# Two mixers' latent section merged into their input projection, with the results taken out of PSUM by ScalarE

## The reference, cut to what matters

```python
proj = h @ w_in                      # 1024 -> c_q 256, c_kv 128, k_r 32, f_q, f_k, f_v 512 each, f_logit 8
q  = (rms_norm(c_q, q_norm_g) @ w_uq).reshape(B, S, 8, 64 + 32)
kv = (rms_norm(c_kv, kv_norm_g) @ w_ukv).reshape(B, S, 8, 64 + 64)
q_rope = rope(q[..., 64:], positions);  k_rope = rope(k_r, positions)
log_f = log_sigmoid(f_logit + fox_forget_b);  F = cumsum(log_f, axis=1)
# then two causal attentions: MLA on q, kv, k_rope; FOX on f_q, f_k, f_v with F[q] - F[k] added
```

## Time and profile before

| | |
|---|---|
| median of 3 runs | 2799.9 us |
| the profiled execution: its own time, and its span | 2798.05 us, 2796.3 us |
| mean granted TensorE clock | 0.943 of full |
| busy: PE, DVE, ACT, POOL | 2484.0, 823.6, 288.8, 15.0 us |
| moved by DMA | 720.37 MB, mean 258 GB/s |

### The profile page before, as it was taken

One profiled execution on the slowest core, in us unless ns is written; L12 is line 12 of the kernel. 1 busy time (PEld: TensorE's weight loads), 2 busy tenths in 40 slices (PEclk: granted clock), 3 DMA queues, 4 the chain that ended last, 5 costly groups with the idle time before them and its releaser, 6 DMA issues. The chain is left out here.

```text
span 2796.3 us, 49835 instructions
## 1 busy us (share of the span) xinstructions
PE 2484.0 (89%) x22580; PEld 1559.8 (56%) x22580; DVE 823.6 (29%) x1418; ACT 288.8 (10%) x588; POOL 15.0 (1%) x12
## 2 busy tenths in 40 slices
PE   4679999977799999999999997799589729999996
PEld 3558888765534445354453534688489524444443
DVE  5672232346301110111011101355363342222222
ACT  1131000103100000000000001331121000000000
POOL 0100000010000000000000000000000000000000
PEclk8889999988799999999999998999699859999998
DMA  8527555503399999999999993333000048999995
GB/s 343 209 118 281 211 218 218 227 1 131 118 381 357 368 369 367 361 380 361 356 370 361 376 359 126 122 137 140 0 19 4 24 173 371 422 422 422 422 422 236
DMA packets 104664, 720.37 MB, mean 258 GB/s; under 512 B 11888, under 2 KB 12560, under 8 KB 29712
## 3 DMA queue, kind: packets, MB, share of 16 engines
q1 hardware_dynamic: 104464, 717.34, 64.8%
HBM read 716.21 MB, written 1.05 MB: 257 GB/s over the span
## 5 line engine op out<-in xcount | busy, mean ns | idle before, releaser
L1316 PE MATMUL bank<-ring,moe_xg 128*32 128x512 f32 (+1 forms) x6144 | 581.9, 539 | 6.1 <-DVE moe_acc L1427 5.5
L1316 PEld LDWEIGHTS bank<-ring,moe_xg 128*32 128x32 f32 x6144 | 198.0, 110 | 378.9 <-issue 368.6
L1340 PE MATMUL bank<-ring,moe_turned 128*32 128x256 f32 x5376 | 296.1, 379 | 0.0
L1340 PEld LDWEIGHTS bank<-ring,moe_turned 128*32 128x32 f32 x5376 | 172.5, 110 | 115.9 <-issue 4.4
L1545 PE MATMUL bank<-ring,moe_shared 128*64 128x512 f32 x1024 | 223.3, 594 | 0.9 <-DVE moe_shared L1599 0.9
L1000 PE MATMUL bank<-h_chan,ring 128*128 128x256 f32 x896 | 197.9, 382 | 3.8 <-ACT h_chan L444 3.8
L1000 PEld LDWEIGHTS bank<-h_chan,ring 128*128 128x128 f32 x896 | 171.8, 192 | 27.9 <-issue 4.1
L1907 PE MATMUL bank<-h_chan,ring 128*128 128x256 f32 x672 | 150.2, 384 | 4.5 <-DVE h_chan L2015 4.5
L1545 PEld LDWEIGHTS bank<-ring,moe_shared 128*64 128x64 f32 x1024 | 72.3, 137 | 142.9 <-issue 142.9
L1439 DVE TENSOR_TENSOR moe_hidden<-moe_silu,bank 128x512 f32<-128x512 f32 (+1 forms) x48 | 26.9, 616 | 400.6 <-PE bank L1316 400.6
L1907 PEld LDWEIGHTS bank<-h_chan,ring 128*128 128x128 f32 x672 | 128.7, 192 | 26.5 <-issue 9.1
(11 more groups left out here) (379 smaller groups left out, 2421.6 us busy)
## 6 DMA issues: line engine op xcount, KB each, us to landing
ring<-stream SPq DMA_DIRECT2D x313, 1024.0 KB, 12.4
ring<-wide SPq DMA_DIRECT2D x240, 1024.0 KB, 7.2
ring<-wide SPq DMA_DIRECT2D x128, 768.0 KB, 6.1
ada_slots<-stream SPq DMA_DIRECT2D x28, 1024.0 KB, 6.9
x_chan<-xT SPq DMA_DIRECT2D x1, 1024.0 KB, 14.7
ring<-lora SPq DMA_DIRECT2D x1, 1024.0 KB, 6.5
out<-x_chan SPq DMA_DIRECT2D x1, 1024.0 KB, 3.9
hyb_work<-dilated SPq DMA_DIRECT2D x1, 768.0 KB, 8.9
```

The costliest lines, as they stand in the source:

```text
L1316: mm = nc.tensor.matmul(banks[r][i * TILE:(i + 1) * TILE, 0:width], xg[:, t, r * TILE:(r + 1) * TILE], w[:, i, :], start=(t == 0), stop=(t ...
L1340: mm = nc.tensor.matmul(sum_bank[r][q * TILE:(q + 1) * TILE, :], turned[:, r, 4 * c + f, i * TILE:(i + 1) * TILE], w[:, f2, q * T:(q + 1) ...
```

## The change

Blocks 1 and 2 become one block. What moves:

- The slots UQ and UKV (query and key/value up-projections) take places 4 and 5 of the stage's stream; the projection's last four slots follow as 6 to 9.
- PE's order is a list of 34 items: 8 projection tiles, 8 query heads, 8 key heads, 2 value tiles, 8 projection tiles, rotating through 5 banks. The sums of squares follow item 4; a rotation product follows each of items 27 to 31, in 2 banks of its own.
- ACT empties all of these banks, and squares the latents straight from PSUM. In its fixed order it takes sine and cosine after item 1, the root after item 5, the forget gate's exponential and logarithm after item 7.
- DVE keeps the norm, the angles, the gate, the variances, the rotation and the modulation. Its modulation slots stand in groups: 0 and 1 behind the angles, 2 and 3 behind the latents' scaling, 4 to 7 behind the gate, 8 to 11 behind the rotation. The two reciprocals become one over 512 elements.
- SP issues positions first, then `c_row`, all mixer slots 2 to 9, modulation slots 4 to 7, the forget sums, modulation slots 8 to 11, and slots 10 to 13.
- POOL's four memsets stand at the start of the merged block.

The diff, cut:

```diff
-        banks = k.bank[1:7]
+        banks, rot_banks, lat_sums = k.bank[1:6], k.bank[6:8], k.bank[0]
+        items = [("tile", j, m) for j in range(4) for m in range(2)]
+        items += [("query", UQ, h) for h in range(HEADS)] + [("key", UKV, h) for h in range(HEADS)]
+        items += [("value", UKV, t) for t in range(TT)] + [("tile", j, m) for j in range(6, 10) for m in range(2)]
...
@@ SP
+                    for j in range(2, 10):
+                        loads.load(sp, j)
+                    for j in range(side.slots, 2 * side.slots):
+                        side.load(sp, j)
                 sp.wait_ge(*S("pool_step").at(2))
                 sp.wait_ge(*forget_step.at(4))
...
+                    for j in range(2 * side.slots, side.n):
+                        side.load(sp, j)
+                    for j in range(10, loads.n):
+                        sp.wait_ge(*side.done(side.n - side.slots + j - 10))
+                        loads.load(sp, j)
@@ PE
+                def turn(i):
+                    pe.wait_ge(*tile_out.at(10 + 2 * i if i < 4 else 4))
+                    if i >= 2:
+                        pe.wait_ge(*rope_ready.at(i - 1))
...
+                for n in range(len(items)):
+                    if n == 8:
+                        pe.wait_ge(*lat_ready.at(2))
+                    if n == 16:
+                        pe.wait_ge(*lat_ready.at(3))
+                    product(n)
+                    if n == 4:
+                        latent_sums()
+                    if 27 <= n < 32:
+                        turn(n - 27)
@@ ACT
+                for n, (kind, j, i) in enumerate(items):
+                    act.wait_ge(*item_done(n))
+                    b = banks[n % NB]
+                    if kind == "query":
+                        a(qm[0:96, i, :], b[0:96, 0:T], ACT.Copy, scale=96 ** -0.5).then_inc(*tile_out.up())
...
+                    elif j < 2:
+                        if n < 3:
+                            a(sq[:, n, :], b[:, 0:T], ACT.Square).then_inc(*lat_squares.up())
...
+                    if n == 1:
+                        act.wait_ge(*S("angle_ready").at(1))
+                        a(sin[:, :], sin[:, :], ACT.Sin)
+                        a(cos[:, :], cos[:, :], ACT.Sin).then_inc(*S("trig_ready").up())
+                    if n == 5:
+                        act.wait_ge(*lat_var.at(1))
+                        a(k.rstd[:, 0:2, :], k.rstd[:, 0:2, :], ACT.Sqrt).then_inc(*lat_root.up())
+                    if n == 7:
+                        act.wait_ge(*forget_step.at(1))
+                        a(e, e, ACT.Exp, scale=-1.0).then_inc(*act_step.up())
...
@@ DVE
+                dve.wait_ge(*S("small_arrived").at(16))
                 dve_angles(k, link, cos, sin, scratch[:, 0, :], scratch[:, 1, :], k.t("freq1"))
+                modulation(0, 1)
+                dve.wait_ge(*tile_out.at(4))
...
+                modulation(2, 3)
...
+                modulation(4, 5)
+                modulation(6, 7)
...
+                modulation(8, 9, 10, 11)
@@ the stream in HBM
+        head = slots_of(np.concatenate([cq, ckv, misc, fq, fk, fv], axis=1))
+        add(head[0:4])
...
+        add(head[4:8])
```

More of the change, by code:

```diff
@@ L564, in stage_mixer, with item_done @@
+        ends = [n + 1 == len(items) or items[n + 1][1] != items[n][1] for n in range(len(items))]
+        def item_done(n):
+            return loads.done(items[n][1]) if ends[n] else tile_done.at(n + 1 - sum(ends[:n]))
+        lat_squares, lat_sum, lat_var = S("squares_ready"), S("sums_ready"), S("var_ready")
+        lat_root, lat_ready = S("lat_root"), S("lat_ready")
+        rot_done, rope_ready = S("rot_done"), S("rope_ready")
         forget_step, forget_moved = S("forget_step"), S("forget_moved")
@@ L632, in _ @@
+                if side is not None:
+                    for j in range(2 * side.slots, side.n):
[3 more added lines that the diff above has]
+                        loads.load(sp, j)
+                loads.rest(sp)
+                sp.wait_ge(*forget_moved.at(32))
             @block.gpsimd
@@ new lines, in _ @@
+                v.scalar_tensor_tensor(e, z, 0.0, lo, ALU.max, ALU.subtract).then_inc(*forget_step.up())
+                dve.wait_ge(*lat_sum.at(1))
+                for g, width in enumerate((256, 128)):
+                    link(v.tensor_scalar(k.rstd[:, g, :], lat_sums[:, g * T:(g + 1) * T], 1.0 / width, EPS, ALU.mult,
+                                         ALU.add))
+                v.reciprocal(k.rstd[:, 0:2, :], k.rstd[:, 0:2, :]).then_inc(*lat_var.up())
+                dve.wait_ge(*lat_root.at(1))
@@ L666, in _ @@
-                n = 0
-                for h in range(HEADS):
-                    dve.wait_ge(*(head_done.at(h + 1) if h < HEADS - 1 else loads.done(8)))
-                    nc.vector.tensor_scalar(qm[0:96, h, :], k.bank[1 + n % 4][0:96, 0:T], 96 ** -0.5, None,
-                                            ALU.mult).then_inc(*head_out.up())
-                    n += 1
-                for h in range(HEADS):
-                    dve.wait_ge(*head_done.at(n))
-                    nc.vector.tensor_copy(km[0:64, h, :], k.bank[1 + n % 4][0:64, 0:T]).then_inc(*head_out.up())
-                    n += 1
@@ L676, in _ @@
-                for t in range(TT):
-                    dve.wait_ge(*(head_done.at(n) if t == 0 else loads.done(9)))
-                    nc.vector.tensor_copy(vm[:, t, :], k.bank[1 + n % 4][:, :]).then_inc(*head_out.up())
-                    n += 1
+                v.tensor_scalar(negF, F, -1.0, None, ALU.mult).then_inc(*forget_step.up())
+                modulation(4, 5)
+                modulation(6, 7)
                 dve.wait_ge(*S("trig_ready").at(1))
-                dve.wait_ge(*head_out.at(8))
```

260 lines of the change are left out of this document (104 added, 156 removed).

## The result

The changed kernel took 2734.53 us (median of 4 runs, 2730.73 to 2735.97) against 2800.97 for the kernel before on the same chip: a ratio of 0.9764, 95% interval 0.9747 to 0.9781. Run again later, 5 times, it took 2734.32, ratio 0.9765 (0.9752 to 0.9778). Forecast were 2730 and a range of 2720 to 2750. The profiled execution took 2735.66 us, its span is 2733.9 (62.4 us shorter), and the mean granted clock went from 0.943 to 0.953. By the medians the gain is 66.4 us: the profiled execution is one of the slower of the four.

What follows compares the result with a forecast made beforehand. Layer 1 was taken as bound by PE, then DVE's chain; layer 0 by SP's order, then the same chain. Gains of 28.4 + 2.4 + 38.7 = 69.5 us off 2798.05 gave 2728.6, as median 2730; range 2720 to 2750.

Steps and rivals of the forecast that it cites:

- PE is the bound of layer 1's merged block: Layer 1's merged block: PE's passes set its length, attention starts at 615.1 instead of 643.47, 28.4 us gained.
- The latents are ready in time: Before item 8 in both mixers: scaled latents ready ahead of PE, with 2.8 us to spare in layer 0, 3.1 in layer 1.
- The short prices of DVE's operations: DVE in the merged block: operations take short times, not 1.9 us beside a memset; otherwise layer 0 loses 1.2 us.
- Item 13 waits 0.6 us: Merged block: PE waits about 0.6 us for item 13's bank while ACT does exponential and logarithm with two table loads.
- The 11.9 us for slots go: Layer 0's projection: PE meets each weight slot as landed, so its 11.9 us of slot waits disappear.
- The rival in which positions and `c_row` wait for eight slots: Layer 0's transfers: both land with the eight slots, 21 us later, latents ready at 85, total 2748; chance 0.07.
- DVE's tail ends layer 0's block, 7 us late: End of layer 0's block: DVE's last four modulation slots end at 117.7, PE at 110.8; attention starts at 118.0.
- Attention of layer 1 gains 2.4 us from its clock: Layer 1's attention: PE arrives at full clock, first 16 passes take 3.5 us instead of 6.93; gain 2.4, bounds 0 and 3.5.
- The size of PE's path: Layer 1's merged block: projection tiles of 3.45 us each plus 17.3 us of passes pushed in between.
- Layer 0: Layer 0's merged block: attention starts at 118.0 instead of 156.77, 38.7 us gained.
- Later stages move as a whole: Dense and mixture stages: they start their loads in block 4, which moves as a whole; rival of no change, 2800, chance 0.02.
- ACT's reads free DVE of 15 us or more in each mixer, which the sums above already use: Both mixers: ACT's new PSUM reads take 15 us or more off DVE, already counted in the block estimates.

Runs made afterwards that it cites:

- the experiment with the spread tail: Changed kernel with layer 0's modulation slot 8 moved before the first rotation step and 9 to 11 between its steps: 2724.72 us, ratio 0.9728.
- the experiment with paired turns: Changed kernel with rotation products two after item 28, two after item 30, one after item 31, instead of one after each of items 27 to 31: 2735.76 us.
- ACT reads twice: Changed kernel with 30 additional reads of PSUM by ACT in each mixer: 2735.60 us, ratio 0.9772.

## Why the prediction was right, and where it was 7 us short

Forecast were 69.5 us off the profiled execution's time; measured were 62.4 (66.4 by the medians, so part of the 7 us is what runs of one kernel differ by). Point by point:

- *PE is the bound of layer 1's merged block.* Right. Item 8 began 535.15 - 503.25 = 31.90 us after PE's start, for which I had 570.1 - 538.2 = 31.9. The block saved 26.3 us instead of 28.4.
- *The latents are ready in time.* Right in both layers: the query latents were scaled at 64.9 in layer 0 and 532.1 in layer 1, 3.1 us before PE's first query head in either (forecast 2.8 and 3.1). The short prices of DVE's operations held.
- *Item 13 waits 0.6 us.* Right, 0.49 in both. By ACT's rows a table load of 1.28 us is followed by its operation after 0.01 (68.98, 70.27). The 5.6 us for table changes in the forecast's range are a term that no run shows; in its place the runs showed this 0.01 us and the wait of 0.49:

```profile
68.98 1.28 ACT L627 ACT_TABLE_LOAD   x1
70.27 0.42 ACT L627 ACTIVATE score<-score 8x256 f32<-8x256 f32 x1
```

- *The 11.9 us for slots go.* Right, and the order of SP is what removes them. The rival in which positions and `c_row` wait for eight slots fell: DVE's cast began at 45.54 and ACT's Silu at 46.82, 1.4 us later than before.
- *DVE's tail ends layer 0's block, 7 us late.* Right: the wait is 7.27 us, for 6.9 and 0.3; the experiment with the spread tail takes those 7 us away.
- *Attention of layer 1 gains 2.4 us from its clock.* Right: 2.6 (33.51 to 30.87), with 1.00 granted from 582.5 to 588.5, and 2.2 in layer 0 where a pause was taken away.
- *The size of PE's path* is the term that was too small. The step "the rotation, 3.9 us" and tiles of 3.45 beside it counted passes only. From the last value product to the last tile, layer 1 took 574.31 + 7.17 - 548.27 = 33.2 us for my 31.5: a turn and the tile behind it take 92.73 - 88.11 = 4.62 us instead of 3.45 + 0.86 = 4.31. The low-rank part took 13.1 instead of 12.7 (0.6 + 6.9 + 3.5 + 1.7). Together 2.1 us in each mixer. In the experiment with paired turns two switches less gave back 0.6, so the five turns make up about 1.5 of the 1.7.
- *Layer 0* was 3.5 us short (35.2 instead of 38.7): these 2.1; 0.7 because PE began 0.7 later; 0.7 because its first five tiles took 19.8 us instead of 19.1. The last two differ from run to run of one code (the changed kernel, run again, began at 36.00 and took 19.50 for 80 passes): the first 80 passes of layer 0's block took 19.15 to 20.23 us in the kernels with this order of SP and the memsets where they were, up to 20.48 with the turns paired, and PE began between 35.7 and 36.8. DVE's tail stands behind the last turn and is later with it.
- *Later stages move as a whole* was nearly right: 63.9 us at the sums after layer 1's attention, 62.4 at the end. Most of the difference arises at the end of layer 1's mixture. The shift is still 63.1 us at its last 16 products with the gates (1720.30 before, 1657.23 after), which follow the same pause of 3.6 us; they took 5.41 us before and 6.48 after, and the next norm's sums are shifted by 61.2 only. No code differs there. Restarts of one code differ by such amounts elsewhere too: behind a pause of 3.9 us, layer 0's first 48 passes of the output projection took 10.60 us in one trace (ACT reads twice), 12.29 in two and 13.0 to 13.3 in seven. Only where the pause was filled is it 10.60 in both mixers.
- *ACT's reads free DVE of 15 us or more in each mixer, which the sums above already use.* Right in size: with DVE taking the results it is busy for 71.9 us in layer 0 instead of 55.1. In layer 1 this room is worth nothing (58.06 us from the sums to attention with DVE's reads, 58.71 with ACT's), and in layer 0 some 6 to 8 us between the two kernels whose modulation slots are spread.

## What to carry to other kernels

Where two blocks are bound by different engines, put the second one's small products between the first one's large ones, and check two orders for it: that the queue brings all weights of the path before anything that waits for side work, and that no side work stands behind the last step of the path. Then price PE by rows with the same neighbours and not by passes: each change to a small product cost it some 0.3 us here (4.62 us for a turn and its tile, not 4.31). After that look at what PE does in each short pause: behind one of 3.6 to 3.9 us the same 48 passes took 10.60 us where 1.00 was granted from the start, and up to 13.46 where 0.50 was granted for the first 5 us, so the lower clock cost from nothing to 2.9 us a time. And where an experiment takes as long as the kernel that it is compared with, ask whether it changes two things that cancel.

## What the runs showed that I had not expected

- Moving 42 reads of PSUM from DVE to ACT was worth nothing in layer 1, and some 6 to 8 us in layer 0 where both kernels spread DVE's modulation slots (2724.72 and 2733.66 us). The equal times of the changed kernel and the one with DVE's reads hid that.
- Behind its first 80 passes layer 1's block repeats to the hundredth: 58.71 us in seven traces. A difference of 0.6 us that no time can tell is plain there.
- ACT's read of 256 columns of PSUM takes 0.38 us alone, but reads in a row start 0.26 to 0.29 us apart; five query heads took 1.47 us in the changed kernel.
- A projection slot behind a transfer that waits for DVE cost more in the merged block (172.58 for attention's start) than in the separate ones (156.77): merging made a loop of what had been a delay.
- The same code restarts differently: the sums of squares behind a pause of 1.88 us took 3.72 (1.00 granted from 154.7 to 158.2 in the changed kernel) or 5.41 (0.53 from 154.7 to 158.0 with the turns paired), the output projection behind one of 3.6 to 3.9 took 10.60 to 13.46. So runs of this kernel, with such pauses in it, differ by some us that no edit explains.
